# Three of sixteen modulation kinds are summed on GpSimd instead of being multiplied on TensorE, one in each of the first three FFNs

## The reference, cut to what matters

```python
mod = (silu(c) @ w_mod[l] + b_mod[l]).reshape(3 * N_SUB, D_MODEL)   # once for c_ctx, once for c
def modulated(j, y):
    return rmsnorm(y, g[j]) * (1 + mod[3 * j + 1]) + mod[3 * j]
x = x + 0.5 * mod[2] * swiglu(modulated(0, x), ffn_w_in[l, 0], ffn_w_out[l, 0])
x = x + mod[5] * mixer(modulated(1, x))
x = x + 0.5 * mod[8] * swiglu(modulated(2, x), ffn_w_in[l, 1], ffn_w_out[l, 1])
```

## Time and profile before

| what | value |
|---|---|
| median of 3 runs | 2351.4 us |
| lowest and highest run | 2349.79, 2352.63 us |
| the profiled execution, its own time | 2348.33 us |
| its span from first to last instruction | 2346.5 us |
| TensorE busy | 2318.9 us, 99% |
| VectorE busy | 1578.9 us, 67% |
| ScalarE busy | 953.6 us, 41% |
| GpSimd busy | 0.2 us |
| granted TensorE clock, mean | 0.998 |
| DMA, mean | 107 GB/s |

### The profile page before, as it was taken

How to read it: one execution, slowest core, us unless ns; L and a number is a source line. 1 busy time by engine, 2 the same in 40 slices (tenths; PEclk the granted TensorE clock), 3 DMA queues, 4 the chain that set the end, 5 groups by cost and what they waited for, 6 DMA issues and landing times.

```text
span 2346.5 us, 39077 instructions
## 1 busy us (share of the span) xinstructions
PE 2318.9 (99%) x16276; PEld 2233.3 (95%) x16276; DVE 1578.9 (67%) x2416; ACT 953.6 (41%) x1501; POOL 0.2 (0%) x4
## 2 busy tenths in 40 slices
PE   7999999999999999999999999999999999999999
PEld 6999999988889999999999999999999999999999
DVE  5886776658867876777587767676345778467463
ACT  6532423443656523424364143244215355234142
POOL 0000000000000000000000000000000000000000
PEclk9999999999999999999999999999999999999999
DMA  8342543421101243334225344225221012322132
GB/s 299 126 144 90 198 162 133 155 89 54 57 19 55 90 162 108 127 126 144 90 74 179 108 156 150 91 77 172 86 75 46 19 55 73 108 72 91 55 99 73
DMA packets 199018, 251.57 MB, mean 107 GB/s; under 512 B 13026, under 2 KB 172602, under 8 KB 198842
## 3 DMA queue, kind: packets, MB, share of 16 engines
q1 hardware_dynamic: 198698, 249.00, 31.7%
q10 hardware_dynamic: 144, 0.07, 0.0%
HBM read 245.76 MB, written 3.28 MB: 106 GB/s over the span
## 4 chain that ended last, share of the span: by engine, by line
PE 87%; DVE 6%; ACT 3%; issue 2%; DMA 1%; SPq 0%; DVEq 0%; ACTq 0%
PE banks L1103 76%; PE banks L1250 1%; PE banks L1427 1%; PE banks L1428 1%; PE banks L1429 1%; DVE w_lo L2620 1%; DMA w_raw<-ffn_w_in 1%; PE banks L1586 1%; DVE w_raw L2641 1%; PE banks L1574 1%; PE banks L1601 1%; ACT w_hi L2029 0%; PE banks L1793 0%; ACT z L2072 0%; PE banks L1967 0%
## 5 line engine op out<-in xcount | busy, mean ns | idle before, releaser
L1103 PE MATMUL banks<-b_hi,w_hi 128*128 128x320 f32 x2496 | 776.7, 311 | 8.5 <-DVE b_lo L2808 3.7
L1103 PE MATMUL banks<-b_hi,w_lo 128*128 128x320 f32 x2496 | 772.2, 309 | 0.0
L1103 PE MATMUL banks<-b_lo,w_hi 128*128 128x320 f32 x2496 | 772.1, 309 | 0.0
L1103 PEld LDWEIGHTS banks<-b_hi,w_hi 128*128 128x128 f32 x2496 | 469.5, 188 | 22.5 <-issue 12.9
L2029 ACT ACTIVATE w_hi<-w_raw 128x1024 fp32r<-128x1024 f32 x296 | 309.8, 1055 | 394.7 <-PE banks L1103 228.5
L1103 PEld LDWEIGHTS banks<-b_lo,w_hi 128*128 128x128 f32 x2496 | 469.5, 188 | 0.0
L1103 PEld LDWEIGHTS banks<-b_hi,w_lo 128*128 128x128 f32 x2496 | 469.4, 188 | 0.0
L2620 DVE TENSOR_TENSOR w_lo<-w_raw,w_hi 128x1024 fp32r<-128x1024 f32 x296 | 361.3, 1223 | 150.1 <-ACT w_hi L2029 148.2
L1103 PE MATMUL banks<-hid_hi,w_hi 128*128 128x320 f32 x1664 | 400.0, 311 | 1.6 <-DVE x L2648 1.1
L1103 PE MATMUL banks<-hid_lo,w_hi 128*128 128x320 f32 x1664 | 396.3, 309 | 0.0
L1103 PE MATMUL banks<-hid_hi,w_lo 128*128 128x320 f32 x1664 | 396.3, 309 | 0.0
(11 more groups left out here) (339 smaller groups left out, 2389.1 us busy)
## 6 DMA issues: line engine op xcount, KB each, us to landing
w_raw<-ffn_w_in SPq DMA_DIRECT2D x176, 512.0 KB, 4.7
mod_grain<-w_mod SPq DMA_DIRECT2D x78, 512.0 KB, 6.1
w_raw<-ffn_w_out SPq DMA_DIRECT2D x64, 512.0 KB, 4.5
last_grain<-w_mod SPq DMA_DIRECT2D x40, 512.0 KB, 5.7
w_raw<-ffn_w_out SPq DMA_DIRECT2D x32, 384.0 KB, 3.6
w_raw<-w_in_odd SPq DMA_DIRECT2D x20, 512.0 KB, 4.6
mod_first<-w_mod SPq DMA_DIRECT2D x3, 2048.0 KB, 15.2
w_raw<-w_in_even SPq DMA_DIRECT2D x12, 512.0 KB, 5.2
```

Of the source, the lines that this page charges most:

```text
L1103: ins = pe.matmul(o, w3[w], v3[v][cols], start=first and i == 0, stop=last and i == 2, skip_group_check=onto_read)
```

## The change

Three kinds of those by products are no longer multiplied on TensorE. Kinds 4, 10 and 15 (one in each of f = 0, 1, 2) are summed on GpSimd, and the others are dealt out anew: kind 5 instead of 6 by VectorE, 7 instead of 8 in the even mixer, 6 in the late windows of f = 0, 8 in two windows of f = 1 after item 1 of doubles 2 and 3. Windows go from 16 to 10: f = 0 loses the four after (5,1), (5,4), (6,1), (6,4), f = 1 loses those at (5,1) and (6,1) and gains those at (2,1) and (3,1), f = 2 loses those at (5,1) and (6,1). VectorE still adds six kinds. TensorE's `acc_sums` runs for nine kinds instead of six; the three new ones come after item 4 of double 7.

A GpSimd kind comes in sixteen pieces, each half a granule (128 x 512, 256 KB), in three half-granule buffers; a fourth half holds a product. For each piece GpSimd multiplies by both vectors (two instructions) and, but for the first granule, adds both products into `mod_acc` (two more): 4 + 4 x 14 = 60 instructions for a kind. It starts when kind 3, 9 or 14 has been summed (after item 1 of double 4). SP issues the sixteen pieces from within the list of weight loads, and pieces from the fourth on wait for GpSimd to be done with the piece three before.

```diff
-        WINDOWS = ({(1, 4): (2, 0), (2, 4): (2, 1), (5, 1): (4, 0), (5, 4): (4, 1), (6, 1): (5, 0), (6, 4): (5, 1),
-                    (9, 1): (7, 0), (9, 4): (7, 1)},
-                   {(5, 1): (10, 0), (6, 1): (10, 1), (9, 1): (12, 0), (10, 1): (12, 1)},
-                   {(2, 1): (13, 0), (3, 1): (13, 1), (5, 1): (15, 0), (6, 1): (15, 1)}, {})
-        MIX_KINDS = (8, 17)
+        WINDOWS = ({(1, 4): (2, 0), (2, 4): (2, 1), (9, 1): (6, 0), (9, 4): (6, 1)},
+                   {(2, 1): (8, 0), (3, 1): (8, 1), (9, 1): (12, 0), (10, 1): (12, 1)},
+                   {(2, 1): (13, 0), (3, 1): (13, 1)}, {})
+        MIX_KINDS = (7, 17)
...
-        ADDED = ({0: 3, 1: 6}, {0: 9, 1: 11}, {0: 14, 1: 16}, {})
-        SUMS_AT = (4, 1), (8, 1)
+        ADDED = ({0: 3, 1: 5}, {0: 9, 1: 11}, {0: 14, 1: 16}, {})
+        POOL_KIND = (4, 10, 15, None)
+        SUMS = ({(4, 1): 3, (7, 4): 4, (8, 1): 5}, {(4, 1): 9, (7, 4): 10, (8, 1): 11}, {(4, 1): 14, (7, 4): 15, (8, 1): 16}, {})
+        PIECES_OF_KIND = [(kt, h) for kt in range(KT) for h in range(2)]
+        PIECE_BUFS = 3
+        PIECE_LOADS = {(3, 1): (0, 3), (4, 1): (3, 7), (5, 0): (7, 8), (5, 1): (8, 12), (6, 0): (12, 13), (6, 1): (13, 16)}
+        POOL_OPS = 2 * 2 + 4 * (2 * KT - 2)
...
+            def load_pieces(f, where):
+                kind = POOL_KIND[f]
+                lay, k = divmod(kind, 3 * N_SUB)
+                for i in range(*PIECE_LOADS[where]):
+                    kt, h = PIECES_OF_KIND[i]
+                    if i < PIECE_BUFS:
+                        used, count = POOL_FREE[kind][i // 2]
+                        sp.wait_ge(used, count)
+                    else:
+                        sp.wait_ge(mod_added, piece_done(f, i - PIECE_BUFS))
+                    c0 = k * D + h * (GRAIN // 2)
+                    sp.dma_start(piece_buf(i), w_mod[lay][:, kt, c0:c0 + GRAIN // 2]).then_inc(mod_in[i % PIECE_BUFS], 16)
...
                         load_in(f, d + 1, 0)
+                        if POOL_KIND[f] is not None and (d, 0) in PIECE_LOADS:
+                            load_pieces(f, (d, 0))
                         load_in(f, d + 1, 1)
+                        if POOL_KIND[f] is not None and (d, 1) in PIECE_LOADS:
+                            load_pieces(f, (d, 1))
...
+        @block.gpsimd
+        def _(pool):
+            def add_kind(f):
+                kind = POOL_KIND[f]
+                pool.wait_ge(mod_used, products_before(kind))
+                pool.wait_ge(acc_summed, added_before(kind))
+                for i, (kt, h) in enumerate(PIECES_OF_KIND):
+                    cols = slice(h * (GRAIN // 2), (h + 1) * (GRAIN // 2))
+                    piece, spare_half = piece_buf(i), grain[3][:, GRAIN // 2:GRAIN]
+                    c_of = [wide_c[:, kt, v:v + 1] for v in range(2)]
+                    pool.wait_ge(mod_in[i % PIECE_BUFS], PIECE_COUNT[kind, i])
+                    before = piece_done(f, i - 1) if i > 0 else adds_before(kind)
+                    if kt == 0:
+                        for v in range(2):
+                            pool.tensor_scalar(mod_acc[:, v, cols], piece, c_of[v], None, ALU.mult).then_inc(mod_added, 1)
+                        continue
...
+                    pool.tensor_scalar(spare_half, piece, c_of[0], None, ALU.mult).then_inc(mod_added, 1)
+                    pool.wait_ge(mod_added, before + 1)
+                    pool.tensor_scalar(piece, piece, c_of[1], None, ALU.mult).then_inc(mod_added, 1)
+                    for v, part in enumerate((spare_half, piece)):
+                        if v == 1:
+                            pool.wait_ge(mod_added, before + 2)
+                        pool.tensor_tensor(mod_acc[:, v, cols], mod_acc[:, v, cols], part, ALU.add).then_inc(mod_added, 1)
```

More of the change, by code:

```diff
@@ L638, in trunk @@
         ODD_GRAINS = (1, 2, 1, 1, 1, 1, 1, 0)
-        ADDED = ({0: 3, 1: 6}, {0: 9, 1: 11}, {0: 14, 1: 16}, {})
-        SUMS_AT = (4, 1), (8, 1)
+        ADDED = ({0: 3, 1: 5}, {0: 9, 1: 11}, {0: 14, 1: 16}, {})
[5 more added lines that the diff above has]
+        POOL_OPS = 2 * 2 + 4 * (2 * KT - 2)
         ADD_OPS = (3, 3, 3, 3, 2, 1, 0, 1)
         HALF_KIND = KT // 2
-        FIRST_WINDOW = ((1, 4), None, (2, 1), None)
-        BY_ADDING = [kind for f in range(4) for kind in ADDED[f].values()]
+        FIRST_WINDOW = ((1, 4), (2, 1), (2, 1), None)
+        BY_ADDING = [kind for f in range(4) for kind in SUMS[f].values()]
         BY_PRODUCTS = [kind for kind in range(FIRST_KIND, DEPTH * 3 * N_SUB) if kind not in BY_ADDING]
@@ L651, in adds_before, with piece_buf, piece_done @@
         def adds_before(kind):
-            return 2 * KT * sum(k < kind for k in BY_ADDING)
+            return sum(POOL_OPS if k in POOL_KIND else 2 * KT for k in BY_ADDING if k < kind)
+        def piece_buf(i):
+            return (grain[2], grain[2], grain[3])[i % PIECE_BUFS][:, (0, GRAIN // 2, 0)[i % PIECE_BUFS]:][:, 0:GRAIN // 2]
+        def piece_done(f, i):
+            return adds_before(POOL_KIND[f]) + (2 * (i + 1) if i < 2 else 4 * (i + 1) - 4)
         def added_before(kind):
@@ L664, in trunk @@
         buf_loads, buf_user = [0] * GRAIN_BUFS, [None] * GRAIN_BUFS
+        POOL_FREE, PIECE_COUNT = {}, {}
         for kind in range(FIRST_KIND, DEPTH * 3 * N_SUB):
+            if kind in POOL_KIND:
+                POOL_FREE[kind] = buf_user[2], buf_user[3]
+                buf_user[0] = buf_user[1] = (acc_summed, added_before(kind) + 1)
+                buf_user[2] = buf_user[3] = (mod_added, adds_before(kind) + POOL_OPS)
+                for i in range(len(PIECES_OF_KIND)):
+                    buf_loads[i % PIECE_BUFS] += 1
+                    PIECE_COUNT[kind, i] = 16 * buf_loads[i % PIECE_BUFS]
+                continue
             for kt in range(GRAIN_BUFS - 1 if kind in MIX_KINDS else KT):
@@ L685, in added_at @@
         def added_at(f, d, t):
-            return ADDED[f].get(SUMS_AT.index((d, t))) if (d, t) in SUMS_AT else None
+            return SUMS[f].get((d, t))
         def kind_done_at(f, d):
@@ L921, in ffn @@
                     if added is not None:
-                        if c == 0 and FIRST_WINDOW[f] is None:
-                            rows_free(f)
                         load_grain(added, 0)
@@ L1267, in acc_sums @@
             def acc_sums(f, kind):
-                pe.wait_ge(mod_added, adds_before(kind) + 2 * KT)
+                pe.wait_ge(mod_added, adds_before(kind) + (POOL_OPS if kind in POOL_KIND else 2 * KT))
                 bank_free(f, kind)
@@ L2594, in _ @@
             act.activation(y_rows[:, 2:TT, LAST_COLS], late_tokens, ACT.Copy).then_inc(x_kept_act, 1)
+        @block.gpsimd
[13 more added lines that the diff above has]
+                            pool.tensor_scalar(mod_acc[:, v, cols], piece, c_of[v], None, ALU.mult).then_inc(mod_added, 1)
+                        continue
+                    if i == 2:
+                        used, count = POOL_FREE[kind][1]
+                        pool.wait_ge(used, count)
+                    else:
+                        pool.wait_ge(mod_added, before - 1)
+                    pool.tensor_scalar(spare_half, piece, c_of[0], None, ALU.mult).then_inc(mod_added, 1)
[5 more added lines that the diff above has]
+                        pool.tensor_tensor(mod_acc[:, v, cols], mod_acc[:, v, cols], part, ALU.add).then_inc(mod_added, 1)
+            for f in range(2 * DEPTH - 1):
+                add_kind(f)
         @block.vector
```

## The result

The changed kernel takes 2440.1 us (median of 4 runs, 2438.07 to 2441.93) against 2350.6 us: the ratio is 1.038, with a 95% interval of 1.037 to 1.040. It is 89.5 us slower. The forecast was slower, 2384 us, with a range to 2430 us: the direction was right, the size was not, and the measured time lies outside the range.

A forecast was written before the change was run, and what follows sets the result against it. TensorE bounds the kernel, with little slack at VectorE's hand-over. Windows gave -9.8 us and exclusion 3 x 14.1: +32.5 on 2348.3 us, 2380.8, or 2384 us as a median; range 2339 to 2430 us.

The forecast's parts named there:

- What bounds the kernel: TensorE, busy 2318.9 of 2346.5 us; VectorE's `c22` hand-over in each double has less than half a microsecond of slack.
- Windows that go: On TensorE, six windows fewer, three sums more and 1.1 us of covered waiting in f = 1: 9.8 us less.
- no change: VectorE still adds six kinds and keeps sixteen; new kinds kept at the end of double 7, hidden in idle time: 0.
- I priced the pieces only by their waits: In SP's queue, same bytes in smaller issues; harm only if GpSimd is not done with an earlier piece in time.
- GpSimd's instructions: From double 4 to 7, 60 instructions a kind take 29 to 73 us, taken as 51, 0.85 us each.
- Rival 3: GpSimd too slow by itself, over 1.4 us an instruction, delays the sum at (7, 4): 2375 us at 1.6; chance 0.11.
- Mutual exclusion: VectorE's two-SBUF-input work, 47.9 us, and GpSimd's 51 us pass one after the other: each stretch at least 14.1 us longer.
- The rule that I weighed: VectorE instructions with two SBUF inputs and GpSimd's SBUF reads need the same port pair; the later waits: the upper bound.
- The estimate by the other page: GpSimd additions take about twice VectorE's time: 28 x 1.2 + 32 x 0.6 = 53 us a kind.
- what piece 12 would do if GpSimd was late: Standing before the next double's load in SP's queue, it would starve the weights, VectorE's sums, then TensorE.
- pieces 8 to 11: Behind `load_in(f, d + 1, 1)` in SP's queue, they can hold back only the next double's loads, about 20 us later.

The follow-up runs named there:

- small-instruction: The changed kernel with GpSimd's 60 instructions a kind working on 8 columns instead of 512, all loads and waits kept; 2349.0 us, ratio 0.9997.
- half: The changed kernel with GpSimd working on granules 0 to 3 of a kind in full and 4 to 7 on 8 columns; 2364.8 us.
- three-quarter: The changed kernel with GpSimd working on granules 0 to 5 of a kind in full and 6 and 7 on 8 columns; 2386.9 us.
- full-addition: The changed kernel with GpSimd's additions on all 512 columns and its products on 8; 2389.0 us, ratio 1.0170.
- the output weights ahead: The complete changed kernel, with SP issuing the first output weights before VectorE's next two granules at the end of double 7; 2425.5 us.
- the kernel with both edits: The changed kernel, GpSimd on 8 columns, only three pieces a kind loaded, VectorE keeping kinds 3, 9 and 14 later in double 5; 2340.9 us.
- the small kernel: A kernel without the trunk, timing GpSimd's products and additions alone and beside VectorE; alone 1.64 us a product, 1.33 us an addition.
- the products and additions apart: Two versions of the changed kernel: products in full with additions on 8 columns, 2350.7 us; the reverse, 2389.0 us.

## Why the prediction was right in direction and wrong in size

*What bounds the kernel.* Right. The hand-over `c22` with less than half a microsecond of slack is where TensorE waits longest in the changed kernel (28.0 us) and in the small-instruction, half, three-quarter and full-addition kernels. With the output weights ahead the sum is (30.0 us).

*Windows that go, 9.8 us.* Right for TensorE by itself (8.5 us in the kernel with both edits, though without 13 of 16 piece loads; 6.3 us with all of them), wrong in the changed kernel's own order: the small-instruction kernel gained nothing. Two steps that I had put at zero failed. I wrote "no change" for VectorE's keeping of kinds and asked only about the new ones; but the keeping of kinds 3, 9 and 14 at the start of double 5 now has no window beside it that occupies TensorE meanwhile. And I priced the pieces only by their waits for a GpSimd that is late, not by what they cost ahead of the weight loads when it is early. Together they ate the saving of 8 us.

*GpSimd's instructions, 29 to 73 us a kind, taken as 51.* This is the main step that failed, and it put the time outside the range: 0.85 us an instruction against 1.50 alone and 1.80 in the kernel. Alone a kind takes 89.7 us. I had bounded GpSimd by VectorE's rows, and had assumed that a product, with one input, is cheaper than an addition; it is dearer, 1.64 against 1.33 us. With 89.7 us, over the 84.9 us of the stretch, GpSimd was late before any contention, by 5 us a kind. Rival 3 (too slow by itself from 1.4 us an instruction) was thus true as well, at 89.7 / 60 = 1.50 us; by itself, on the prediction's terms, it would have given 3 x 4.8 - 9.8 = +5 us, and +14 with the saving that did not arrive, so lateness without contention is not the main cause. No run has GpSimd late and VectorE undisturbed.

*Mutual exclusion.* Right in kind, and shown by the small kernel and by the products and additions apart. As a sum it was too simple, in the other direction: 47.9 + 89.7 = 137.6 us "one after the other" would have made the stretch 53 us longer, and it became 25.3 us longer. Products hold VectorE back little, though they wait for it themselves; additions and VectorE exclude one another nearly. The errors ran against one another: with the measured 89.7 us the prediction's own sum would have given a loss of 3 x 52.7 - 9.8 = 148 us, so it is luck that the forecast came within 56 us. The direction is not luck: half of GpSimd's work, never late, costs 15.8 us. In the stretch of f = 0 VectorE lost 23 x 0.25 + 12 x 0.35 + 6 x 0.39 + 6 x 0.49 = 15 us, and GpSimd 110.2 - 89.7 = 20.5 us. The rule that I weighed (the Trainium skill, SBUF — State Buffer, Who interferes with whom) nearly agrees with the small kernel's trace for additions (31.1 us against 34.3 one after the other) and goes too far for products (28.1 against 38.0). The estimate by the other page (the Trainium skill, GPSIMD Engine Reference, Performance versus the Vector engine) was 53 us a kind. What it states of additions comes near: 1.33 us measured against 0.61 on VectorE. The 0.6 us that I took for a product is not the double of VectorE's 0.37 either, and the product took 1.64 us; that is where the 53 us fail.

*Two terms missing from the sum.* The first is SP's queue. The prediction had named what piece 12 would do if GpSimd was late, but with 0.85 us an instruction it never was; and it held that pieces 8 to 11 could only delay loads 20 us later; piece 11 did just that. SP's timeline in double 6 of f = 0 and VectorE's wait behind it:

```profile
270.91 0.33 SPq L925 DMA_DIRECT2D last_grain<-w_mod  x1
271.34 0.93 SPq L891 DMA_DIRECT2D w_raw<-ffn_w_in  x2
277.81 0.34 SPq L925 DMA_DIRECT2D mod_grain<-w_mod  x1
278.19 0.98 SPq L891 DMA_DIRECT2D w_raw<-ffn_w_in  x2
```
```profile
284.23 1.23 DVE L2713 TENSOR_TENSOR w_raw<-w_raw 128x1024 f32<-128x1024 f32 x1 [3.84 <-DMA w_raw<-ffn_w_in]
```

Pieces 11 and 12 go out the moment GpSimd frees their buffers, each weight load right behind its piece, and VectorE waits 3.84 us for the second. I had also not seen the granules at the end of double 7, which wait for GpSimd's last addition with the output weights behind them: 14.6 us in all. The second is the clock, which falls after TensorE has waited: some 3 us in the stretch of f = 0, and some 4 us right behind it (319.5 to 335).

*How the loss adds up.* By medians: 2349.0 us with the saving already spent; +15.8 for the first half of GpSimd's work; +22.1 up to three quarters; +53.2 for the last quarter, where GpSimd is late for the sum: 2440.1. Of the 53.2, the order of the output weights brings 14.6 back.

TensorE's own record divides it by what TensorE did. From the small-instruction kernel to the changed one the profiled spans grow by 89.8 us (2346.5 to 2436.3): 23.8 us more busy time for the same matmuls (2314.6 to 2338.4), much of it at the low clock (some 7 us in f = 0); 20.3 us more waiting for `c22` (7.7 to 28.0); 25.3 us for the sum; and 20.1 us for ScalarE's parts. That makes 89.5. So lateness at the sum itself is about a quarter of the loss, and what TensorE loses in waits for VectorE and ScalarE and by the clock is the larger part.

No complete version here beats the kernel before. The most that the exchange could bring, with GpSimd's full work at no cost, is 6.3 us with all loads in place and 8.5 without most of the pieces; and the additions, 28 a kind, cost 13 us a kind.

## What to carry to other kernels

An engine that looks idle is worth what its instructions take on it: time one product and one addition alone and beside the neighbour before planning a deadline, and do not bound them by another engine's rows. Look for the hand-over with the least slack, not for the mean load, and ask of removed TensorE work what it was covering. A load that waits for a slow engine belongs in a queue in which nothing urgent stands behind it.

## What the runs showed of the hardware that was not expected

- On GpSimd a product of one SBUF input and a per-partition scalar takes 1.64 us for 128x512, longer than an addition of two SBUF inputs (1.33 us); a plain copy takes 5.33 / 8 = 0.67 us.
- A GpSimd addition of two SBUF inputs holds VectorE's two-input instructions off, 12.7 us for 12 additions; products hold them off for 3.3 us, for the 8 that ran beside them, but took 2.69 us each there instead of 1.64. Beside VectorE instructions with one PSUM input GpSimd is not delayed (1.65 and 1.34 us), and those take 0.60 us each beside products, beside additions and in the 1.75 us in which GpSimd was done.
- After waits of TensorE the granted clock fell to 1.2 GHz for parts of what followed: the five microseconds after GpSimd's last addition ran at a mean of 0.55 of full clock, after 9.5 us in which TensorE had waited.
